# Tails ahead of the new pair's scores in the stick-breaking stage of a two-block transformer kernel

## What is computed

```python
z = jnp.einsum("bhtd,bhsd->bhts", qb, kb) * scale
causal = s_idx < t_idx
log_not = jnp.where(causal, jax.nn.log_sigmoid(-z), 0.0)
tail = lax.cumsum(log_not, axis=3, reverse=True) - log_not
log_a = jax.nn.log_sigmoid(z) + tail
a = jnp.where(causal, jnp.exp(log_a), 0.0)
outs.append(jnp.einsum("bhts,bhsd->bhtd", a, vb))
```

## Time and profile before

| | |
|---|---|
| median of 3 runs | 2240.02 us (2239.84 to 2243.54) |
| profiled execution | 2245.55 us |
| its span, first to last instruction | 2243.8 us |
| mean granted TensorE clock in it | 0.996 |
| TensorE busy, whole span | 2212.6 us (99%) |
| VectorE, ScalarE, GpSimd busy | 926.5, 834.6, 959.2 us (41%, 37%, 43%) |
| chain that ended last | PE 91%, DVE 5%, POOL 2% |

### The profile page before, as it was taken

One profiled execution on the slowest core, in us unless ns is written; L12 is line 12 of the kernel. 1 busy time (PEld: TensorE's weight loads), 2 busy tenths in 40 slices (PEclk: granted clock), 3 DMA queues, 4 the chain that ended last, 5 costly groups with the idle time before them and its releaser, 6 DMA issues.

```text
span 2243.8 us, 28104 instructions
## 1 busy us (share of the span) xinstructions
PE 2212.6 (99%) x10348; PEld 1756.8 (78%) x10349; DVE 926.5 (41%) x1324; ACT 834.6 (37%) x1394; POOL 959.2 (43%) x434
## 2 busy tenths in 40 slices
PE   9999999999999999999999999999999899999998
PEld 7888888885557888888878888888877568888886
DVE  4111346568755211244763411134552754111344
ACT  5222226435863322223632422222443654222223
POOL 5444444561005544444534444444343534444443
PEclk9999999999999999999999999999999999999999
DMA  5223232441002322323322222222222002322222
GB/s 192 94 97 105 97 112 96 140 140 38 1 1 76 112 93 100 105 94 113 107 81 94 87 102 93 93 94 98 90 94 76 20 29 87 110 93 93 94 94 75
DMA packets 31340, 202.64 MB, mean 90 GB/s; under 512 B 3616, under 2 KB 5280, under 8 KB 7584
## 3 DMA queue, kind: packets, MB, share of 16 engines
q1 hardware_dynamic: 29904, 197.68, 25.6%
q10 hardware_dynamic: 1360, 3.93, 0.6%
HBM read 198.45 MB, written 2.10 MB: 89 GB/s over the span
## 4 chain that ended last, share of the span: by engine, by line
PE 91%; DVE 5%; POOL 2%; issue 1%; ACT 1%; DMA 0%; POOLq 0%; SPq 0%; DVEq 0%; ACTq 0%
PE PS L1094 28%; PE PS L1096 28%; PE PS L1095 27%; PE PS L1501 1%; PE PS L1544 1%; PE PS L1576 1%; PE PS L1390 1%; DVE NMAX L2054 1%; DVE PS L1826 0%; POOL XL L545 0%; DVE XL L1698 0%; PE PS L1374 0%; POOL WL L505 0%; PE PS L1230 0%; POOL X L537 0%
## 5 line engine op out<-in xcount | busy, mean ns | idle before, releaser
L505 POOL TENSOR_TENSOR WL<-RAW,WH 128x1024 fp32r<-128x1024 f32 x365 | 895.6, 2458 | 1203.7 <-ACT WH L589 1203.5
L1094 PE MATMUL PS<-XH,WH 128*128 128x512 f32 (+1 forms) x2166 | 844.1, 390 | 1.9 <-DVE XL L1698 0.7
L1096 PE MATMUL PS<-XH,WL 128*128 128x512 f32 (+1 forms) x2166 | 836.6, 386 | 0.0
L1095 PE MATMUL PS<-XL,WH 128*128 128x512 f32 (+1 forms) x2166 | 836.2, 386 | 0.0
L589 ACT ACTIVATE WH<-RAW 128x1024 fp32r<-128x1024 f32 x365 | 384.1, 1059 | 1172.8 <-PE PS L1096 1134.3
L1094 PEld LDWEIGHTS PS<-XH,WH 128*128 128x128 f32 x2166 | 406.8, 188 | 90.0 <-issue 5.3
L1096 PEld LDWEIGHTS PS<-XH,WL 128*128 128x128 f32 x2166 | 406.8, 188 | 83.2
L1095 PEld LDWEIGHTS PS<-XL,WH 128*128 128x128 f32 x2166 | 407.0, 188 | 82.1 <-issue 1.7
L1094 PE MATMUL PS<-HHL,WH 128*128 128x512 f32 x672 | 261.4, 389 | 0.0
L1095 PE MATMUL PS<-HHL,WH 128*128 128x512 f32 x672 | 261.4, 389 | 0.0
L1096 PE MATMUL PS<-HHL,WL 128*128 128x512 f32 x672 | 261.4, 389 | 0.0
(11 more groups left out here) (249 smaller groups left out, 1609.8 us busy)
## 6 DMA issues: line engine op xcount, KB each, us to landing
RAW<-wstream SPq DMA_DIRECT2D x183, 1024.0 KB, 4.9
X<-xT SPq DMA_DIRECT2D x8, 256.0 KB, 5.5
WORK<-memT ACTq DMA_DIRECT2D x2, 1024.0 KB, 6.0
RAW<-wstream SPq DMA_DIRECT2D x4, 256.0 KB, 5.1
outT<-WORK SPq DMA_DIRECT2D x4, 256.0 KB, 3.0
PB<-WORK ACTq DMA_DIRECT2D x8, 127.8 KB, 2.4
CST<-consts SPq DMA_DIRECT2D x1, 827.0 KB, 9.6
outT<-WORK ACTq DMA_DIRECT2D x3, 256.0 KB, 3.6
```

The source lines that it names most:

```text
L505: pool.tensor_tensor(WL[:, s, :, :].rearrange("p a b -> p (a b)"), RAW[:, s, :], WH[:, s, :, :].rearrange("p a b -> p (a b)").bitcast(F), ...
L1094: pe.matmul(o, wh, xh, start=start, stop=False)
L1095: pe.matmul(o, wh, xl, start=False, stop=False)
L1096: return pe.matmul(o, wl, xh, start=False, stop=stop)
```

## The change

In each round from t = 6 on, TensorE issues the two tails first, then the new pair, then the value products. No instruction is added or taken away, no wait is changed, and the lists of the other engines and all DMAs stay as they were.

```diff
             for t in range(SB_AHEAD, n + LAG_V, 2):
-                if SB_AHEAD < t < n:
-                    sb_pair(t)
                 if 0 <= t - LAG_T < n:
                     sb_tail(t - LAG_T)
                     sb_tail(t + 1 - LAG_T)
+                if t < n:
+                    sb_pair(t)
                 if t == SB_AHEAD:
-                    sb_pair(t)
                     flip(JOBS["kv"][-1])
                 if t == LAG_V:
                     pe.wait_ge(turned, FLIPS[max(FLIPS)]["c"])
```

## The result

The changed kernel took 2288.65 us (median of 4 runs, 2288.02 to 2290.24), the kernel before 2241.02 on the same chip. The ratio is 1.0202 with a 95% interval of 1.0189 to 1.0215. By the two medians the change costs 47.6 us where 38.5 were predicted. The profiled execution took 2288.02 us with a span of 2286.2 and a mean granted clock of 0.988 (before: 2245.55, 2243.8 and 0.996). The page still shows TensorE busy for 98% of the span, and a chain that is 89% TensorE, 5% VectorE and 2% GpSimd, where it was 91, 5 and 2: as before, the whole hides the stage.

The account below looks back on a forecast made before the run. No engine is full in the 85.5 us stage; waits between engines set its time. 30.4 + 1.1 + 0 + 7 = 38.5 on the 2240.0 median (profiled run 5.5 above) gave 2278.5; range 2267 to 2296, low end widened by 3.

Parts of the forecast that it names:

- the ring: One-round loop: masks, clip, rounding, clip, rounding, GpSimd subtraction, second tail, next pair; 19.56 us a turn instead of 13.47.
- Item 1 of the sum: Five turns from the pair at 1745.98 to the last: 99.4 us instead of 68.96, +30.4.
- the 1.6 us of GpSimd's weight units: Extra in the first turn, where GpSimd has two weight units to split; kept in both sums.
- Item 2: First moved pair comes behind two tails of 256 columns: +1.1 us, bounds 0 and 1.5.
- Item 3: Way from the last pair to the stage's end, the same list as before: 0.
- Item 4: Granted clock falls in the longer stage as TensorE idles more: +7 us, bounds 0 and 38.
- seven falls: Clock falls expected in ten places, two long rounds in each of five turns, at 1.0 us each.
- the low-clock rival: TensorE stays at 1.2 GHz for most of the stage: 2310 us; chance 0.08.
- The rivals on the other side: Tails fill the scores' wait, up to 18.0 us gone, 2222, chance 0.03; no ring, even exchange, 2240, chance 0.03.
- the ring 10% too long: Case for the range's low end: no clock fall and a ring read too long, 2240 + 27 = 2267.
- The signs: Turn 19 to 21 us, tails' idle at least triples, scores' idle nearly gone, other engines' busy unchanged, clock below 0.98.
- Before and behind the stage nothing moves: Profile sign: outside the 85.5 us stage that the change touches, nothing shifts.

Follow-up runs that it names:

- Two cuts on VectorE: Changed kernel with the older pair's rounding ahead of the newer clip, 2261.63 us; the same with the unrounded softplus also ahead of the clip, 2253.65 us.
- one on TensorE: Kernel before with the new pair between the two tails from t = 6, VectorE's order old: 2257.53 us, ratio 1.0063.

## Why the prediction was right, and where it was off

**The bound and the ring: right.** TensorE's place behind `sb_lo` of the pair's older neighbours closes a ring of one round. Three of the four rounds ran at full clock in the changed kernel and stand 0.02 to 0.03 us from the predicted ones; the fourth, 5.82 with zero matmuls in the gaps, is 0.11 off, and the whole turn with the clock held is 19.72 against 19.56. Two cuts on VectorE and one on TensorE shortened it by 3.2, 4.6 and 4.0 us, where 3.2, 4.8 and 5.0 were worked out.

**Item 1 of the sum, +30.4: 29.6 by the trace.** The ring's five turns are 0.8 longer than predicted (5 x 0.16), and the 1.6 us of GpSimd's weight units that I kept did not show. The tail that waits for them in the first turn waited 0.39 us, as the tail in the same place of the last turn did. That a fall took their place in the first turn (clock 0.77) is possible; with the zero matmuls the wait behind them was 1.49. What they cost by themselves was not tried.

**Item 2, the first pair, +1.1: 1.6,** just above its upper bound of 1.5.

**Item 3, the end, 0: +1.5,** by the clock again. Before had one fall of 3.4 us behind its last pair, the changed kernel has one of 6.8, and with the zero matmuls and no fall there the same way took 11.48 us instead of 12.98.

**Item 4, the clock, +7: this term was mis-sized.** The step that failed is "seven falls" of 3.4 us at 1.0 each, with the length of a fall taken from the one in the earlier trace rows. There were six falls in the stage, five of them in the turns, a count that was nearly right. But four of them lasted 10.2 us, one 6.8 and one 3.4, some 51 us in all. Together they cost up to 13.4 in the turns, 2.7 a fall and not 1.0, and 1.5 behind them. Stretches of one of them, columns as in the earlier trace rows:

```profile
1772.20:1782.50 10.30, 9.13 (x36) 6.64 (x34) 2.48 (x6) 2.10 (x6) 2.54 (x2) 0.50 0.00 0
1774.00:1776.50 2.50, 1.33 (x7) 0.33 (x5) 2.32 (x6) 1.46 (x5) 1.27 (x1) 0.50 0.00 0
1776.50:1782.00 5.50, 5.50 (x20) 4.87 (x20) 0.16 (x1) 0.65 (x2) 1.27 (x1) 0.50 0.00 0
```

In the earlier trace rows TensorE was busy all 3.4 us behind the fall, and the clock came back. In the changed kernel the ring goes on at the low clock: the four long falls began at the tails of 384 columns and lasted through the wait ahead of the tails of 512 (TensorE idles 1.17 of the 2.50 us in the second row), into these tails or just behind them. Such a fall slowed the pair and the tails on the way, which are on the ring. What ends a fall is not shown. It is not simply the next run without a gap: in the fence the clock stays low through 5.5 us of it, and with the zero matmuls TensorE was busy in all of the 10.2 us of the one fall. The argument that TensorE is busier at the low clock, which I held against the low-clock rival, was right in that the clock came back in each turn, and wrong about how soon. That rival said 2310, with the low clock in most of the stage; it was some 51 of 131.6 us, and the time lies 21 us below the rival's and 10 above mine.

**The rivals on the other side** are out. The tails did not fill the scores' wait: no scores waited for ScalarE any more, but the tails waited far longer for GpSimd. The size of that rival was also misread. The 18.0 us of the earlier trace rows and the 12.4 of the earlier trace rows add idle weight loads to idle matmuls. By matmuls TensorE idled 85.50 - 76.43 = 9.1 us in the whole stage of before, of which 2.2 + 1.4 = 3.6 lay ahead of the scores and 5.2 ahead of the tails, where the changed kernel has 31.1 (the view of waits of before, columns as above):

```profile
PE PS L1390 <- POOL XL L545: 5.2, 8, 1.2
...
PE PS L1374 <- ACT WORK L1046: 2.2, 5, 0.4
PE PS L1374 <- ACT PB L1046: 1.4, 1, 1.4
```

So work put into the scores' wait had some 4 us of idle matmul time to fill, and not 18. The forecast does not use these 18.0 us. The Trainium skill (Perfetto Trace Analysis, Optimization Strategy) names a lack of free PSUM as one possible reason for a gap that repeats, and the earlier trace rows agree, since the scores waited for a bank; it does not say that other work put into such a gap is a gain, and here it was a loss of 47.6. What the Trainium skill says on matmuls in batches (Perfetto Trace Analysis, Matmul Optimizations) agrees with the trace: the clock of the stage was 0.81 with the gaps, and 1.00 from the third turn on where zero matmuls filled them.

**The range.** Its low end was worked out too high: "the ring 10% too long" took 10% off the added 30.4 us, where 10% of five turns of 19.56 is 9.8, and 2240 + 30.4 - 9.8 is 2261 and not 2267.

**The signs.** The tails' idle time rose sixfold, the scores' is gone, and the other engines' busy time is unchanged, all as promised. The turn was said to be 19 to 21 us; it was 21.1 to 23.0, by the clock. "Before and behind the stage nothing moves" did not hold: the stage starts at 1738.8 instead of 1742.4. Two stretches of before show why (columns as in the earlier trace rows), and the first one in the changed kernel, in the second fence.

```profile
601.00:608.00 7.00, 6.87 (x40) 3.96 (x39) 4.27 (x17) 4.21 (x20) 0.00 (x0) 0.54 0.00 0
615.00:618.00 3.00, 3.00 (x13) 1.59 (x14) 0.62 (x4) 1.73 (x6) 0.00 (x0) 0.55 0.00 0
```

```profile
601.00:608.00 7.00, 6.69 (x56) 3.80 (x54) 5.83 (x24) 5.80 (x27) 0.00 (x0) 1.00 0.00 0
```

In that execution of before, the clock had fallen twice in an earlier attention; in that of the changed kernel it had not, with the same program there. The prediction scaled 5.5 us off without asking what they were; most of them are these two falls, which cost 3.6 us.

## What to carry to other kernels

When a step is moved behind a wait on an in-order engine, follow what that wait needs through the other engines' lists, back to the step itself: if a list holds "newer first, older second", the move can close a ring, and its length can be read from one turn of the old trace (here 19.56 us, measured 19.72). Shorten such a ring at any of its engines, and look for the same order where it does not bind yet: rounding ahead of clip was worth 27 us inside the ring, some 16 of them without the clock, and still 4 in the kernel before. Do not take the length of a fall of the clock from a single one: here they lasted from 3.4 to 10.2 us, and what ended them stayed open. And before waiting time is called a gain to be had, compare it with the engine's idle time by matmuls.

## What the runs showed of the hardware that was not expected

The granted clock fell to 1.2 GHz, six times, in a stage whose longest gap ahead of a tail was 1.9 us. It stayed there for up to 10.2 us, with matmuls on TensorE for about 9 of them, and with zero matmuls in the gaps it stayed there once for 10.2 us in which TensorE had no gap by the modelled ends of its matmuls. And it differs between executions of the same instructions: 0.54 in one of them and 1.00 in the other over the same 7 us, 1100 us ahead of the change.
